# GpSimd makes the low parts of three of the 18 weight units of each expert

## The chip, the cores and the metric

The kernel runs on one core of one Trainium2 chip. The metric is the device time of one execution in microseconds (us), median of several runs. The core has five engines that run side by side and meet through semaphores: TensorE (PE, with its weight loads shown apart as PEld), VectorE (DVE), ScalarE (ACT), GpSimd (POOL) and SyncE (SP, whose queue issues the weight transfers). All arithmetic here is in 32-bit floats.

## The reference

The reference is two transformer blocks over 256 tokens of width 1024. The first block has attention and a dense feed-forward network. The second runs two layers of a hybrid mixer; after the first mixer comes a dense network, after the second a mixture of experts. The change touches that last stage alone:

```python
logits = (x @ router_w).astype(jnp.float32) + router_b.astype(jnp.float32)
top_vals, top_idx = lax.top_k(logits, TOP_K)              # TOP_K = 2 of N_EXPERTS = 8
top_w = jax.nn.softmax(top_vals, axis=-1)
gate = jnp.sum(jax.nn.one_hot(top_idx, N_EXPERTS, dtype=jnp.float32) * top_w[..., None], axis=-2)
out = jnp.zeros_like(x)
for e in range(N_EXPERTS):                                # F_EXPERT = 1408
    out = out + gate[..., e:e + 1] * swiglu(x, w1[e], w3[e], w2[e])
```

where `swiglu(x, w1, w3, w2)` is `(silu(x @ w1) * (x @ w3)) @ w2`.

## The kernel before, in words

**How a product keeps its precision.** Every operand of a matrix product is split into a high part, which TensorE's fast 32-bit format holds exactly, and a low part, the rest. A product is three matmuls: high by high, low by high and high by low (lines 1369 to 1371). ScalarE makes the high part of a weight with a copy (`split_moe` of the scalar engine, line 730), VectorE the low part with a subtraction, raw minus high (`split_moe` of the vector engine, line 1262).

**The units of an expert.** The weights of one expert come in 18 units. Units 0 to 11 are gate and up weights in three chunks of columns, two gate halves and two up halves for each chunk (0 to 3, 4 to 7, 8 to 11). Units 12 to 17 are the down weights, two column halves of three parts. A unit has 2048 columns for each of 128 partitions; units 8 to 11, 14 and 17 have 1536.

**The rings.** Raw weights land in a ring of six places (`RAW_MOE`; three are shown as `raw`, three as `scr`). The high and the low parts have rings of four places each (`W_MOE`; shown as `w_hi` and `w_lo`, and the fourth place as `mt_hi` and `mt_lo`). SP issues the load of unit m, two transfers, once the low part of unit m-6 is made, since then the raw place is free (lines 394 and 395). ScalarE makes the high part of unit m when the load has landed and TensorE has used unit m-4. VectorE makes the low part of m as soon as the high part is there. TensorE waits for the low part of m on the counter `lo_ready` and multiplies (`rows` for units 0 to 11, `down` for 12 to 17).

**The order around the change.** Every engine has the order of its work written out by hand. Within expert e, VectorE does the splits of units 4, 5 and 6, then `gate_up(0)` (line 1280: the activation times the up product), splits 7 and 8, `take_hidden(0)` (line 1292: low part of the turned hidden rows), splits 9 and 10, the next expert's rows (`take_rows`, line 1267), `gate_up(1)`, splits 11 and 12, `take_hidden(1)`, splits 13 and 14, `take_rows`, `gate_up(2)`, splits 15 and 16, `take_hidden(2)`, split 17, `take_y(0)` (line 1305), then splits 0, 1 and 2 of the next expert, `take_y(1)`, and split 3. TensorE multiplies units 0 to 4, turns the hidden rows (`turn_hidden(0)`, line 1834), multiplies 5 and 6, turns half of the next expert's tokens (`turn_gathered`, line 1770), multiplies 7 and 8, `turn_hidden(1)`, 9 and 10, then waits for `take_hidden(1)` and turns the second half of the tokens, then 11, 12, `turn_hidden(2)`, 13, waits for `take_hidden(2)`, and 14 to 17.

**GpSimd before.** In this stage its queue holds the indirect transfer that gathers the tokens of each expert (line 458), and after the last one the load of the gain and bias of the final normalisation (`load_norm(6)`, line 418), which waits until the last expert's tokens are turned. The final normalisation uses them on line 864.

**Sparse and dense.** An expert with at most 128 tokens runs with one tile of gathered tokens, one with more runs over both tiles of all 256 tokens. Each engine reads the count and branches at the start of an expert. In this data seven experts are sparse and expert 6 is dense.

Of the kernel before, what the change touches and what calls it, by code (L numbers as in the profile page):

```python
# [21 lines left out]
F32 = mybir.dt.float32  # L22
F32R = mybir.dt.float32r
U32 = mybir.dt.uint32
ALU = mybir.AluOpType
# [10 lines left out]
EXPERTS = 8  # L36
# [3 lines left out]
RING = 3  # L40
# [13 lines left out]
U_MOE = U_MIX[1] + 27  # L54
# [8 lines left out]
PER_EXPERT = len(EXPERT_UNITS)  # L63
RAW_MOE = 2 * RING
W_MOE = RING + 1
FT = F_EXPERT // P


def unit_width(m):
    kind, c, part = EXPERT_UNITS[m % PER_EXPERT]  # L70
    return DOWN_TILES[part][1] * 512 if kind == "D" else 4 * CHUNKS[c][1]
# [71 lines left out]
def two_blocks(nc, A, const_dram, out):  # L143
    with ExitStack() as ctx:
# [61 lines left out]
        raw_moe = [raw[:, (U_MOE + k) % RING, :] for k in range(RING)] + [area(at, UNIT) for at in (0, 2048, 4096)]  # L206
# [92 lines left out]
        def ev(name):  # L299

            if name not in S:
                S[name] = sem(name)
            return S[name]
# [15 lines left out]
            eng.wait_ge(evacuated[q % 2], q // 2 + 1)  # L319


        def k_major(w):
            return w.rearrange("(k p) n -> p k n", p=P)

        @block.sync
        def _(sp):
            for t in range(TT):
                sp.dma_start(x[:, t, :], A["x"][0, t * P:(t + 1) * P, :]).then_inc(x_landed[t], 16)
            sp.dma_start(ident, const_dram[:, 0:P]).then_inc(ev("ident_landed"), 16)

            def load(u, slot, first, second, width=1024):

                if not (isinstance(u, int) and u < RING):
                    sp.wait_ge(lo_ready, u - RING + 1)
                fill(raw[:, slot, :], raw_landed[slot], first, second, width)

            def fill(place, landed, first, second, width):
                for half, src in ((0, first), (1, second)):
                    dst = place[:, half * width:(half + 1) * width]
                    if len(src.shape) == 3:  # L340
                        dst = dst.rearrange("p (k n) -> p k n", k=src.shape[1])
                    elif len(src.shape) == 4:
                        dst = dst.rearrange("p (e k n) -> p e k n", e=src.shape[1], k=src.shape[2])
                    sp.dma_start(dst, src).then_inc(landed, 16)

            def load_square(u, w, c):
                v = k_major(w)
                load(u, u % RING, v[:, 0:4, c:c + 256], v[:, 4:8, c:c + 256])

            def load_short(u, w, c):  # L350
                v = k_major(w)
                load(u, u % RING, v[:, 0:2, c:c + 512], v[:, 2:4, c:c + 512])

            def load_ffn(u0, wg, wu, wd):
                gv, uv = k_major(wg), k_major(wu)
                with sp.Fori(0, FT_DENSE // 2) as i:
                    for j in range(2):
                        c = bass.ds(i * 256 + j * P, P)
                        load(u0 + j + i * 3, (u0 + j) % RING, gv[:, :, c], uv[:, :, c])
                    load(u0 + 2 + i * 3, (u0 + 2) % RING, wd[bass.ds(i * 256, P), :], wd[bass.ds(i * 256 + P, P), :])  # L360

            for n, (_, c) in enumerate(IN1):
                load_square(U_IN1 + n, A["w_in"][0], c)
            for n in range(4):
                load_square(U_WO + n, A["w_o"][0], n * 256)
            load_ffn(U_FFN1, A["w_gate"][0], A["w_up"][0], A["w_down"][0])
            for l in range(2):
                for n in range(19):
                    load_square(U_MIX[l] + n, A["w_in_2"][l], n * 256)
                for n in range(2):  # L370
                    load_short(U_MIX[l] + 19 + n, A["w_o_attn_2"][l], n * 512)
                for n in range(2):
                    load_short(U_MIX[l] + 21 + n, A["w_o_ret_2"][l], n * 512)
                for n in range(4):
                    load_square(U_MIX[l] + 23 + n, A["w_out_2"][l], n * 256)
                if l == 0:
                    load_ffn(U_FFN2, A["ffn_w1_2"][0], A["ffn_w3_2"][0], A["ffn_w2_2"][0])
            for m in range(PER_EXPERT * EXPERTS):
                e, (kind, c, part) = m // PER_EXPERT, EXPERT_UNITS[m % PER_EXPERT]
                if m < RING:  # L380
                    sp.wait_ge(lo_ready, U_MOE + m - RING + 1)
                elif m == RING:
                    sp.wait_ge(ev("routing"), 1)
                elif m >= RAW_MOE:
                    sp.wait_ge(lo_ready, U_MOE + m - RAW_MOE + 1)
                if kind == "D":
                    at, n = DOWN_TILES[part]
                    v = k_major(A["moe_w2_2"][0, e])[:, at:at + n, c * 512:(c + 1) * 512]
                else:
                    at, n = CHUNKS[c]  # L390
                    v = k_major(A["moe_w1_2" if kind == "G" else "moe_w3_2"][0, e])[:, 4 * part:4 * part + 4, at:at + n]
                rows, width = v.shape[1], v.shape[2]
                dst = raw_moe[m % RAW_MOE][:, 0:rows * width].rearrange("p (k n) -> p k n", n=width)
                sp.dma_start(dst[:, 0:2], v[:, 0:2]).then_inc(raw_moe_landed[m % RAW_MOE], 16)
                sp.dma_start(dst[:, 2:], v[:, 2:]).then_inc(raw_moe_landed[m % RAW_MOE], 16)

            for t in range(TT):
                sp.wait_ge(rows_ready, 2 * 6 + t + 1)
                sp.dma_start(out[0, t * P:(t + 1) * P, :], x[:, t, :]).then_inc(stored, 16)
            sp.wait_ge(stored, 16 * TT)  # L400
# [3 lines left out]
        def _(pool):  # L404
# [46 lines left out]
            for t in range(TT):  # L451
                pool.wait_ge(x_stored[t], 16)
            pool.wait_ge(gb_used, 6)
            for e in range(EXPERTS):
                pool.wait_ge(ev("slots_ready"), 1 if e == 0 else 2)
                if e >= 2:
                    pool.wait_ge(x_turned, 2 * (e - 1))
                pool.indirect_dma_start(x_rows[:, e % 2, :], None, x_dram, bass.IndirectOffsetOnAxis(slot_token[:, e:e + 1], 0)) \
                    .then_inc(rows_gathered[e % 2], 16)
            pool.wait_ge(x_turned, 2 * EXPERTS)  # L460
            load_norm(6)

# [356 lines left out]
        def _(dve):  # L819
# [435 lines left out]
            dve.wait_ge(ev("counts_ready"), 1)  # L1255

            def split_moe(m):
                if m >= PER_EXPERT * EXPERTS:
                    return
                s, width = m % W_MOE, unit_width(m)  # L1260
                dve.wait_ge(hi_ready, U_MOE + m + 1)
                TTo(wl_moe[s][:, 0:width], raw_moe[m % RAW_MOE][:, 0:width], wh_moe[s][:, 0:width].bitcast(F32), ALU.subtract).then_inc(lo_ready, 1)  # L1262
# [102 lines left out]
        def _(pe):  # L1365
# [417 lines left out]
            def expert(e, dense):  # L1783
# [8 lines left out]
                def rows(p):  # L1792

                    kind, c, half = EXPERT_UNITS[p]
                    n, s = CHUNKS[c][1], (e * PER_EXPERT + p) % W_MOE
                    bank = 0 if kind == "G" else (2 if dense else 1)
                    if half == 0 and kind == "G":
                        if c == 0:
                            pe.wait_ge(xg_ready, 2 * e + 2)
                        if e or c:  # L1800
                            pe.wait_ge(silued, 3 * e + c)
                        if e and c == 0 and dense:
                            pe.wait_ge(y_ready, 2 * e)
                    if half == 0 and kind == "U" and (e or c):
                        pe.wait_ge(hid_rows, 3 * e + c)
                        if dense:
                            pe.wait_ge(hid_pair, 3 * e + c)
                        if c == 0:
                            pe.wait_ge(y_ready, 2 * e)
                    pe.wait_ge(lo_ready, u + p + 1)  # L1810
                    for t in range(tiles):
                        tok = slice(t * P, (t + 1) * P)
                        for k in range(4):
                            w = slice(k * n, (k + 1) * n)
                            last = product(ps[:, bank + t, 0:n], xh[4 * half + k][:, tok], xl[4 * half + k][:, tok],
                                           wh_moe[s][:, w], wl_moe[s][:, w], half == 0 and k == 0, half == 1 and k == 3)
                    last.then_inc(unit_used, 1)
# [19 lines left out]
                def down(p):  # L1837
# [1 line left out]
                    _, c, part = EXPERT_UNITS[p]  # L1839
                    s = (e * PER_EXPERT + p) % W_MOE  # L1840
                    first, n = DOWN_TILES[part]
                    pe.wait_ge(lo_ready, u + p + 1)
                    pe.wait_ge(hid_pair, 3 * e + part + 1)
                    if e and not dense and part == 0 and c == 0:
                        pe.wait_ge(y_ready, 2 * e)
# [87 lines left out]
```

## Time and profile before

| what | value |
|---|---|
| median of 3 runs | 1581.41 us (1580.67 to 1583.89) |
| the profiled execution | 1578.89 us |
| its span in the trace | 1577.1 us |
| mean granted TensorE clock | 0.948 of full speed |
| PE busy | 1417.8 us (90% of the span) |
| VectorE busy | 972.1 us (62%) |
| ScalarE busy | 776.3 us (49%) |
| GpSimd busy | 38.1 us (2%) |
| the expert stage | about 1062 to 1562 us of the span |

The span is the time from the first to the last instruction of the trace; the execution's own time is 1.8 us more. Busy time counts computing instructions only, and matmuls overlap, so that a busy TensorE isn't one at its peak. A row of a timeline gives start, duration, engine, line, output and inputs; in square brackets stands the idle time of that engine just before it and what ended it.

### The profile page before, as it was taken

The numbers are of one execution on the slowest core, as the hardware profiler recorded it, in microseconds if no ns is written. First come the engines' busy times: TensorE is split into PE (matmuls) and PEld (weight loads), VectorE is DVE, ScalarE is ACT, GpSimd is POOL, SyncE is SP. The second block draws the span as 40 slices with busy tenths as digits, with TensorE's granted clock in tenths as the row PEclk, the third lists the DMA queues.
The fourth block names the chain that finished last, engine by engine and source line by source line (L and its number), as shares of the span: only waits on it lengthen the run. The fifth ranks groups of instructions, "written<-read, shape, count | busy, mean of one in ns | idle before, by whom it ended". The sixth has DMA issues, their size and how long they took to land.

```text
span 1577.1 us, 21924 instructions
## 1 busy us (share of the span) xinstructions
PE 1417.8 (90%) x8969; PEld 1282.8 (81%) x8969; DVE 972.1 (62%) x953; ACT 776.3 (49%) x784; POOL 38.1 (2%) x59
## 2 busy tenths in 40 slices
PE   4996899997999988999979999869999999889975
PEld 4985899996999977999969998757777777778864
DVE  5585654556446775455564467658688888664556
ACT  3663345443554433445436454317566666544353
POOL 1000000001000000000000000010000000000000
PEclk9997999998999998999979999969899999999998
DMA  8432466665445345656644443368899999775761
GB/s 255 160 108 54 134 186 187 185 186 140 137 155 153 112 138 148 193 170 183 198 129 140 149 151 96 121 226 288 273 359 318 321 328 346 256 259 172 235 192 63
DMA packets 249343, 299.84 MB, mean 190 GB/s; under 512 B 10016, under 2 KB 180128, under 8 KB 249120
## 3 DMA queue, kind: packets, MB, share of 16 engines
q1 hardware_dynamic: 244688, 283.22, 55.5%
q0 software_dynamic: 4560, 15.27, 3.5%
q8 instruction: 70, 1.15, 0.3%
q14 instruction: 25, 0.20, 0.0%
HBM read 296.35 MB, written 2.10 MB: 189 GB/s over the span
## 4 chain that ended last, share of the span: by engine, by line
PE 79%; DVE 14%; ACT 4%; issue 2%; DMA 1%; SPq 0%; ACTq 0%; DVEq 0%
PE ps L1369 21%; PE ps L1370 20%; PE ps L1371 20%; DVE w_lo L1262 3%; PE ps L1564 3%; PE ps L1565 3%; PE ps L1566 3%; ACT w_hi L730 2%; DVE w_lo L826 1%; DMA raw<-in_w_in_dram 1%; PE ps L1653 1%; PE ps L1634 1%; DVE x L864 1%; DVE x L865 1%; DVE small L839 1%
## 5 line engine op out<-in xcount | busy, mean ns | idle before, releaser
L826 DVE TENSOR_TENSOR w_lo<-raw,w_hi 128x2048 fp32r<-128x2048 f32 x139 | 317.9, 2291 | 232.7 <-ACT w_hi L474 232.7
L474 ACT ACTIVATE w_hi<-raw 128x2048 fp32r<-128x2048 f32 x139 | 264.9, 1907 | 192.8 <-PE ps L1371 119.0
L1369 PE MATMUL ps<-xt_hi,w_hi 128*128 128x256 f32 x912 | 263.2, 289 | 15.8 <-DVE xt_lo L875 15.8
L1370 PE MATMUL ps<-xt_lo,w_hi 128*128 128x256 f32 x912 | 262.0, 287 | 0.0
L1371 PE MATMUL ps<-xt_hi,w_lo 128*128 128x256 f32 x912 | 261.6, 287 | 0.0
L1369 PE MATMUL ps<-w_hi,xt_hi 128*128 128x256 f32 (+3 forms) x808 | 240.8, 298 | 5.8 <-DVE xt_lo L835 3.1
L1370 PE MATMUL ps<-w_lo,xt_hi 128*128 128x256 f32 (+3 forms) x808 | 237.7, 294 | 0.0
L1371 PE MATMUL ps<-w_hi,xt_lo 128*128 128x256 f32 (+3 forms) x808 | 237.7, 294 | 0.0
L1369 PEld LDWEIGHTS ps<-xt_hi,w_hi 128*128 128x128 f32 x912 | 179.2, 197 | 19.7 <-issue 18.8
L1370 PEld LDWEIGHTS ps<-xt_lo,w_hi 128*128 128x128 f32 x912 | 179.3, 197 | 0.8
L1371 PEld LDWEIGHTS ps<-xt_hi,w_lo 128*128 128x128 f32 x912 | 179.1, 196 | 0.0
L1369 PEld LDWEIGHTS ps<-w_hi,xt_hi 128*128 128x128 f32 x808 | 157.6, 195 | 12.0 <-issue 6.3
L1370 PEld LDWEIGHTS ps<-w_lo,xt_hi 128*128 128x128 f32 x808 | 157.7, 195 | 2.0
L1371 PEld LDWEIGHTS ps<-w_hi,xt_lo 128*128 128x128 f32 x808 | 157.6, 195 | 2.1
L1262 DVE TENSOR_TENSOR w_lo<-raw,w_hi 128x2048 fp32r<-128x2048 f32 (+1 forms) x57 | 121.8, 2141 | 39.1 <-ACT w_hi L730 38.7
L1262 DVE TENSOR_TENSOR w_lo<-scr,w_hi 128x2048 fp32r<-128x2048 f32 (+1 forms) x48 | 99.3, 2069 | 72.2 <-ACT w_hi L730 72.2
L730 ACT ACTIVATE w_hi<-raw 128x2048 fp32r<-128x2048 f32 (+1 forms) x57 | 102.0, 1794 | 44.7 <-PE ps L1371 44.7
L730 ACT ACTIVATE w_hi<-scr 128x2048 fp32r<-128x2048 f32 (+1 forms) x48 | 83.3, 1736 | 74.3 <-PE ps L1371 74.3
L1369 PE MATMUL ps<-w_hi,xg_hi 128*128 128x512 f32 (+1 forms) x252 | 98.6, 391 | 20.5 <-issue 18.7
L1370 PE MATMUL ps<-w_lo,xg_hi 128*128 128x512 f32 (+1 forms) x252 | 96.8, 384 | 0.0
L1371 PE MATMUL ps<-w_hi,xg_lo 128*128 128x512 f32 (+1 forms) x252 | 96.5, 383 | 0.0
L592 ACT ACTIVATE scr<-ps 128x256 f32<-128x256 f32 x44 | 16.9, 384 | 121.5 <-PE ps L1371 121.5
(350 smaller groups left out, 2453.5 us busy)
## 6 DMA issues: line engine op xcount, KB each, us to landing
raw<-in_moe_w_dram SPq DMA_DIRECT2D x120, 512.0 KB, 5.2
raw<-in_w_in_dram SPq DMA_DIRECT2D x100, 512.0 KB, 4.7
scr<-in_moe_w_dram SPq DMA_DIRECT2D x88, 512.0 KB, 6.6
raw<-in_ffn_w_dram SPq DMA_DIRECT2D x66, 512.0 KB, 4.3
scr<-in_moe_w_dram SPq DMA_DIRECT2D x48, 384.0 KB, 3.9
raw<-in_w_gate_dram SPq DMA_DIRECT2D x22, 512.0 KB, 4.0
raw<-in_w_up_dram SPq DMA_DIRECT2D x22, 512.0 KB, 5.2
raw<-in_w_down_dram SPq DMA_DIRECT2D x22, 512.0 KB, 4.2
```

The costliest lines, as they stand in the source:

```text
L474: A_(w_hi[:, slot, :], raw[:, slot, :], ACT.Copy).then_inc(hi_ready, 1)
L592: A_(silu_t[:, j, :], ps[:, (s0[1] + j) % 2, 0:T], ACT.Silu).then_inc(silu_ready, 1)
L730: A_(wh_moe[s][:, 0:width], raw_moe[k][:, 0:width], ACT.Copy).then_inc(hi_ready, 1)
L826: TTo(w_lo[:, slot, :], raw[:, slot, :], w_hi[:, slot, :].bitcast(F32), ALU.subtract).then_inc(lo_ready, 1)
L839: return nc.vector.bn_stats(stats[:, t, c, :], x[:, t, c * 512:(c + 1) * 512])
L1262: TTo(wl_moe[s][:, 0:width], raw_moe[m % RAW_MOE][:, 0:width], wh_moe[s][:, 0:width].bitcast(F32), ALU.subtract).then_inc(lo_ready, 1)
L1369: MM(dst, a_hi, b_hi, start=start, stop=False)
L1370: MM(dst, a_hi, b_lo, start=False, stop=False)
L1371: return MM(dst, a_lo, b_hi, start=False, stop=stop)
L1564: MM(dst, h_hi_t[:, j, tok], w_hi[:, s, w], start=False, stop=False)
L1565: MM(dst, h_hi_t[:, j, tok], w_lo[:, s, w], start=False, stop=False)
L1566: last = MM(dst, h_lo_t[:, j, tok], w_hi[:, s, w], start=False, stop=False)
```

## The change

VectorE no longer makes the low parts of units 5, 11 and 17 of each expert; GpSimd makes them, with the same subtraction. They count on a semaphore of their own (`pool_low`), and SP and TensorE wait for the one or the other by a new helper. On GpSimd's queue the gather of the tokens of expert e+1 now stands in front of the three subtractions of expert e, and so behind those of expert e-1; before it only waited for tokens to be turned. Reads and writes are the same data in the same places.

```diff
+POOL_LOW = (5, 11, 17)
+
+def by_pool(m):
+    return RING < m < PER_EXPERT * EXPERTS and m % PER_EXPERT in POOL_LOW
+
+def low_count(m):
+
+    return sum(by_pool(i) == by_pool(m) for i in range(m + 1))
...
+        def wait_low(eng, m):
+
+            if by_pool(m):
+                eng.wait_ge(ev("pool_low"), low_count(m))
+            else:
+                eng.wait_ge(lo_ready, U_MOE + low_count(m))
...
                 elif m >= RAW_MOE:
-                    sp.wait_ge(lo_ready, U_MOE + m - RAW_MOE + 1)
+                    wait_low(sp, m - RAW_MOE)
...
-            for e in range(EXPERTS):
+            def fetch_rows(e):
                 pool.wait_ge(ev("slots_ready"), 1 if e == 0 else 2)
                 if e >= 2:
                     pool.wait_ge(x_turned, 2 * (e - 1))
                 pool.indirect_dma_start(x_rows[:, e % 2, :], None, x_dram, bass.IndirectOffsetOnAxis(slot_token[:, e:e + 1], 0)) \
                     .then_inc(rows_gathered[e % 2], 16)
+
+            def split_low(m):
+                s, width = m % W_MOE, unit_width(m)
+                pool.wait_ge(hi_ready, U_MOE + m + 1)
+                nc.gpsimd.tensor_tensor(wl_moe[s][:, 0:width], raw_moe[m % RAW_MOE][:, 0:width],
+                                        wh_moe[s][:, 0:width].bitcast(F32), ALU.subtract).then_inc(ev("pool_low"), 1)
+
+            fetch_rows(0)
+            for e in range(EXPERTS):
+                if e + 1 < EXPERTS:
+                    fetch_rows(e + 1)
+                for k in POOL_LOW:
+                    split_low(e * PER_EXPERT + k)
             pool.wait_ge(x_turned, 2 * EXPERTS)
             load_norm(6)
...
             def split_moe(m):
-                if m >= PER_EXPERT * EXPERTS:
+                if m >= PER_EXPERT * EXPERTS or by_pool(m):
                     return
...
-                    pe.wait_ge(lo_ready, u + p + 1)
+                    wait_low(pe, e * PER_EXPERT + p)
```

The last pair of lines stands twice, in `rows` and in `down`.

## Rows read from the trace of the kernel before

**Rows 1.** The page: busy time of each engine, and the chain by engine.
```profile
PE 1417.8 (90%) x8969; PEld 1282.8 (81%) x8969; DVE 972.1 (62%) x953; ACT 776.3 (49%) x784; POOL 38.1 (2%) x59
PE 79%; DVE 14%; ACT 4%; issue 2%; DMA 1%; SPq 0%; ACTq 0%; DVEq 0%
```

**Rows 2.** Waits of TensorE, 1062 to 1562 us: total, times, longest.
```profile
PE ps L1369 <- issue: 19.5, 9, 8.3
PE ps L1369 <- DVE h_lo_m L1292: 12.6, 7, 1.8
```

**Rows 3.** Chain that ended last, 1200 to 1218 us: start, duration, what.
```profile
1202.14 1.93 ACT w_hi L730
...
1204.09 2.29 DVE w_lo L1262
1206.39 0.61 DVE h_lo_m L1292
...
1207.04 0.66 PE ps L1770 x4
```

**Rows 4.** Timeline of expert 2 around its unit 11: ScalarE, then VectorE.
```profile
1200.05 1.49 ACT L730 ACTIVATE mt_hi<-scr 128x1536 fp32r<-128x1536 f32 x1 [1.27 <-PE ps L1371]
1201.58 1.76 DVE L1262 TENSOR_TENSOR mt_lo<-scr,mt_hi 128x1536 fp32r<-128x1536 f32 x1 [0.23 <-ACT mt_hi L730]
```

**Rows 5.** Timeline of expert 2: high part of unit 5, low part of 6, then.
```profile
1181.90 1.91 ACT L730 ACTIVATE w_hi<-scr 128x2048 fp32r<-128x2048 f32 x1
1187.14 2.29 DVE L1262 TENSOR_TENSOR w_lo<-raw,w_hi 128x2048 fp32r<-128x2048 f32 x1 [1.00 <-ACT w_hi L730]
1189.35 0.74 DVE L1280 SCALAR_TENSOR_TENSOR const<-ps,small,scr 128x512 f32<-128x512 f32 x1
1190.53 0.60 PE L1834 MATMUL ps<-const 128*128 128x128 f32 x4
```

**Rows 6.** The queue of GpSimd: timeline.
```profile
1.94 0.56 POOL L421 MEMSET zeros<- 128x512 f32 x1
1057.67 2.78 POOL L458 DMA_INDIRECT gb<-x_dram,slot_token  x1 [4.75 <-DVE slot_token L1254]
1061.10 0.94 POOL L458 DMA_INDIRECT gb<-x_dram,slot_token  x1 [0.65 <-issue]
1154.64 1.59 POOL L458 DMA_INDIRECT gb<-x_dram,slot_token  x1 [58.91 <-PE ps L1770]
```

**Rows 7.** VectorE beside two of those transfers: timeline.
```profile
1057.30 2.29 DVE L1262 TENSOR_TENSOR mt_lo<-scr,mt_hi 128x2048 fp32r<-128x2048 f32 x1
1153.13 2.29 DVE L1262 TENSOR_TENSOR mt_lo<-raw,mt_hi 128x2048 fp32r<-128x2048 f32 x1
```

**Rows 8.** Expert 0 around its unit 5: ScalarE, VectorE, TensorE.
```profile
1068.96 1.91 ACT L730 ACTIVATE w_hi<-scr 128x2048 fp32r<-128x2048 f32 x1
1073.11 2.29 DVE L1262 TENSOR_TENSOR w_lo<-raw,w_hi 128x2048 fp32r<-128x2048 f32 x1
L1834 PE MATMUL ps<-const x4: 272/272/273, 1076.2 to 1076.5; 128*128 128x128 f32 x4
```

**Rows 9.** Dense expert 6: VectorE's low parts of its units 6 and 12.
```profile
1421.94 2.29 DVE L1262 TENSOR_TENSOR w_lo<-raw,w_hi 128x2048 fp32r<-128x2048 f32 x1 [3.27 <-ACT w_hi L730]
1454.23 2.29 DVE L1262 TENSOR_TENSOR w_lo<-raw,w_hi 128x2048 fp32r<-128x2048 f32 x1 [2.85 <-ACT w_hi L730]
```

**Rows 10.** Expert 2: high part of unit 17, VectorE's first split behind it.
```profile
1215.81 1.48 ACT L730 ACTIVATE w_hi<-scr 128x1536 fp32r<-128x1536 f32 x1 [0.84 <-PE ps L1371]
1222.34 2.29 DVE L1262 TENSOR_TENSOR w_lo<-raw,w_hi 128x2048 fp32r<-128x2048 f32 x1 [1.11 <-ACT w_hi L730]
```

**Rows 11.** Chain that ended last, 1530 to 1577 us: start, duration, what.
```profile
1544.06 4.44 DVE w_lo L1262 x2
...
1568.70 1.30 DVE x L864
```

**Rows 12.** Transfers of 1175 to 1229 us: count, KB each, us to landing.
```profile
scr<-in_moe_w_dram SPq DMA_DIRECT2D x11, 512.0 KB, 6.9
```

More of the change, by code:

```diff
@@ L1841, in down @@
                     first, n = DOWN_TILES[part]
-                    pe.wait_ge(lo_ready, u + p + 1)
+                    wait_low(pe, e * PER_EXPERT + p)
                     pe.wait_ge(hid_pair, 3 * e + part + 1)
```

## The prediction

> **What bounds the kernel now.** I read the page first: TensorE is busy 90% of the span, VectorE 62%, GpSimd 2%, and 79% of the chain that ended last is TensorE [rows 1]. A lighter VectorE is worth something only where TensorE waits for it. The waits of TensorE in the expert stage show where: each of the seven sparse experts has one wait of up to 1.8 us for line 1292, the low part of the turned hidden rows; the rest is mostly "issue", at the starts of experts [rows 2]. The chain inside one expert then shows what stands ahead of such a wait: high part of unit 12, 1202.14 to 1204.07, its low part from 1204.09 to 1206.38, line 1292, and TensorE again at 1207.04 [rows 3]. The reader is to see that the low part of unit 12 starts 0.02 us after its high part has ended: VectorE was waiting for ScalarE, and ScalarE for TensorE to free a place of the ring. The last step was to look at what VectorE does just before it: the low part of unit 11 (one of the three that move) ends at 1203.34, and VectorE is then idle for 0.75 us [rows 4]. It is the same for unit 5: the low part of unit 6 has 1.00 us of idle time before it, ended by ScalarE [rows 5]. And VectorE's first split behind unit 17 is preceded by 1.11 us of idle time [rows 10].
>
> So what is taken off VectorE was followed by a pause each time, and no row has TensorE waiting because of it. The removal itself is worth nothing.
>
> **The change part by part.** *Removed:* 24 subtractions on VectorE, three per expert: one of 2048 columns (2.29 us) and two of 1536 (1.76 us), 5.81 us per expert, 46 us in all. On the path: 0, by the above.
>
> *Added: the price of one split on GpSimd.* The trace shows no two-input operation there. Below, it can't be expected to beat VectorE's own 2.29 us by a row. The nearest GpSimd row is the clearing of 128x512 in 0.56 us [rows 6], 1.09 ns per column for one stream. Three streams, one after another (two read, one written), would be 2048 x 3 x 1.09 ns = 6.69 us; two, if the write goes along with the reads, 4.46 us. I take 4.46 us, that row's rate once for each of the two inputs; it also lies in the middle of 2.29 and 6.69. For 1536 columns three quarters: 3.34 us, bounds 1.76 and 5.02.
>
> *Is such a split late by itself?* Unit 11: its high part ends at 1201.54, GpSimd would end at 1204.9; TensorE can't use it before the turning at 1207.04 is over [rows 3, 4]. With 5.02 us it would be 1206.6, still in time. Unit 5: high part done at 1183.81, GpSimd ends at 1188.3, at worst at 1190.5; TensorE comes to it after the turning that starts at 1190.53 [rows 5]. Unit 17: high part done at 1217.29, GpSimd done at 1220.6 [rows 10], while four units of down weights stand between it and its use. None is late.
>
> *Does it hold up VectorE?* This is the term that decides. When the kernel before asks GpSimd for an indirect transfer, which reads its list of rows from the on-chip memory, its duration depends on VectorE. With no split running it is 0.94 us (1061.10). Issued at 1057.67, while VectorE subtracts from 1057.30 to 1059.59, it takes 2.78 us and ends at 1060.45, which is 0.86 us behind the end of that subtraction. Issued at 1154.64, during the one from 1153.13 to 1155.42, it takes 1.59 us and ends 0.81 us behind [rows 6, 7]. Six such issues stand beside a split and all end 0.8 to 0.9 us after it. GpSimd's read waits, then, until the whole two-input subtraction is over. I take it that the wait works the other way round too: a subtraction of VectorE that comes while GpSimd subtracts starts when GpSimd has finished. VectorE's other work here (lines 1280, 1292, 1267, 1305) has one input in the accumulators and I count it as free.
>
> The Trainium skill, "SBUF — State Buffer", section "SBUF: two separate sides", says it outright: VectorE and GpSimd share a pair of ports under an exclusive lock, the first holds it for its whole instruction, and a VectorE operation with two inputs in that memory needs it against a GpSimd operation that reads. The rows show one direction of this; no row shows VectorE as the one that waits. The "GPSIMD Engine Reference", section "Elementwise — side-by-side cycle accounting", states 4497 ns for a two-input operation of 2048 columns; by that the sum below would be 13.5 instead of 13.0 us.
>
> *Unit 11.* GpSimd starts at 1201.58 and ends at 1204.92. The low part of unit 12 would start at 1204.09, so it is held for 0.83 us, and it is on the chain: line 1292 and TensorE's turning move by 0.83 us. Expert 7 turns no further tokens, but there the chain runs through VectorE's queue behind the same split, down to the splits that end at 1548.50 [rows 11], so it pays the same. Seven sparse experts: 7 x 0.83 = 5.8 us.
>
> *Unit 5.* GpSimd works from 1183.85 to 1188.31; the low part of unit 6 is due at 1187.14 and held for 1.17 us. Queued behind it on VectorE is line 1280, now 1189.35 to 1190.09, then 1190.52 to 1191.26. TensorE's turning waits for that: with some 0.1 us of handing over it starts at 1191.36 instead of 1190.53 [rows 5], 0.83 us late. Six experts: 5.0 us. In expert 0 the high part of unit 5 comes late, at 1070.87, so GpSimd holds until 1075.36 and the low part of unit 6 is late by 2.25 us; the turning follows its line 1280 with 0.1 us of room [rows 8]: 2.2 us.
>
> *Unit 17.* GpSimd is done at 1220.6, and the next split of VectorE is due at 1222.34 [rows 10]: 0.
>
> *Dense expert 6.* TensorE takes twice as long per unit, and the low parts of units 6 and 12 stand behind 3.27 and 2.85 us of idle time [rows 9], that is 5.56 and 4.61 us behind the starts of 5 and 11, more than 4.46 and 3.34: 0.
>
> *Moved.* SP's loads wait for the low parts. The load of unit 11 goes out 2.2 us later (4.46 against 2.29). Before, it was issued when unit 5 was done, at about 1186.1, lands in 6.9 us [rows 12] and is wanted at 1200.05 [rows 4]: 7 us of room. The two narrow ones move by 1.6 us. Behind it in SP's queue stand the loads of the following units with the same room. The gathers of tokens come up to an expert later, behind unit 17 of the expert before; each moves 128 rows of 4 KB, 512 KB, as much as one transfer that lands in 6.9 us [rows 12], and the rows are turned from the seventh unit of the next expert on, some 20 us later. The final gain and bias now wait for unit 17 of expert 7. VectorE's splits of 15 and 16 end at 1548.50 there, unit 17 follows on GpSimd from about 1549.0 to 1552.4, and with 1.2 us of issue and 7 us of landing the rows are there at 1560.6, wanted at 1568.70 [rows 11]. All 0, with 8 us of room in the last; that room is gone only if GpSimd takes three times what I think.
>
> *Sum.* 5.8 + 5.0 + 2.2 = 13.0 us slower. On the profiled execution (span 1577.1, own time 1578.89) that is 1591.9; the median of the runs is 2.5 us above it, 1581.41, and 1594.4 is what I forecast.
>
> **The rivals.** *A, no blocking:* GpSimd's subtraction doesn't hold up VectorE's. For it: the rows show only GpSimd waiting, never VectorE. Against it: the wait in the one direction is for a whole instruction, which looks like a lock. Then every term above is 0 and the time is 1581.4. This is the case on the other side (not slower); it decides at the first split of unit 12. *B, blocking, and GpSimd takes 6.69 and 5.02 us:* unit 11 holds unit 12 until 1206.60, 2.51 us, seven times, 17.6; unit 5 holds unit 6 for 3.40, of which 0.34 is hidden, 3.06 six times, 18.4; expert 0 pays 4.4. Together 40.4, 1621.8. *C, the two share:* VectorE's split is only slowed while both run, say by half of what I price: 6.5 us, 1587.9. *D, faster:* TensorE's waits at expert starts are uneven, up to 8.3 us and 19.5 us in nine of them [rows 2]; if the later gathers leave these starts quieter, a few us come back, 5 perhaps, which only shows as faster if nothing blocks: 1576.4.
>
> **How the numbers follow.** The forecast has 0.62, A 0.17, C 0.08, B 0.06, D 0.07. What a measurement of this kernel can tell is about 0.2%, 3.2 us. My own forecast reaches from 1589 to 1603: a price of 4.0 to 5.0 us, a tenth of a us of handing over at each of 14 stalls, and stretches at TensorE's lower clock, whose granted mean is 0.948 and which longer pauses could make more frequent. A lies inside the range and B mostly outside: 1580.5 to 1604. Slower by over 0.2%: the forecast, B and C, less what of C and the forecast falls short, 0.73. Within 0.2%: A and that remainder, 0.19. Faster: D and a bit of A, 0.08.
>
> **What would show it.** In the profile after: 24 rows of GpSimd of about 4.5 and 3.3 us; in the sparse experts the low part of unit 12 starts not 0.02 but about 0.85 us after its high part, right at the end of GpSimd's split; the wait for line 1292 before the turning of tokens grows by 0.8 us; TensorE waits for line 1280 before the first turning of hidden rows. The forecast is wrong if VectorE's splits overlap GpSimd's with their usual 2.29 us (A), or if one of GpSimd's is the last thing that TensorE waits for (B).

## The result, and the profile after

The changed kernel takes 1598.62 us (median of 7 runs, 1591.84 to 1602.39), the kernel before in the same sittings 1581.41 (7 runs, 1571.87 to 1590.22). The ratio is 1.0102, with a 95% interval from 1.0066 to 1.0138: slower by 16 us, give or take 6. The profiled execution has a span of 1597.8 us, 20.7 more than before.

The page after: busy times and the chain by engine, beside [rows 1]. VectorE lost 30 us of busy time where 46 were taken off it; the other 16 are waits that count as busy, as the timeline below shows. GpSimd went from 38 to 128.5 us, and the chain has less TensorE and more VectorE.

```profile
PE 1424.2 (89%) x8969; PEld 1286.6 (81%) x8969; DVE 941.9 (59%) x929; ACT 777.3 (49%) x784; POOL 128.5 (8%) x83
PE 75%; DVE 15%; ACT 5%; issue 4%; DMA 1%; SPq 0%; ACTq 0%; DVEq 0%
```

GpSimd's new work, two of its four groups by shape and place: count, total us, mean ns. A whole unit takes 4.65 us, a narrow one 3.51.

```profile
L484 POOL TENSOR_TENSOR w_lo<-scr,w_hi 128x1536 fp32r<-128x1536 f32 x8 | 28.1, 3511 | 122.7 <-ACT w_hi L763 122.7
L484 POOL TENSOR_TENSOR mt_lo<-scr,mt_hi 128x2048 fp32r<-128x2048 f32 x4 | 18.6, 4650 | 96.6 <-ACT mt_hi L763 96.6
```

Timeline of expert 2 of the changed kernel, first around unit 5, then around unit 11; it answers to [rows 4, 5].

```profile
1188.41 4.66 POOL L484 TENSOR_TENSOR w_lo<-scr,w_hi 128x2048 fp32r<-128x2048 f32 x1 [16.98 <-ACT w_hi L763]
1191.67 3.55 DVE L1295 TENSOR_TENSOR w_lo<-raw,w_hi 128x2048 fp32r<-128x2048 f32 x1 [4.24 <-ACT w_hi L763]
1195.14 0.74 DVE L1313 SCALAR_TENSOR_TENSOR const<-ps,small,scr 128x512 f32<-128x512 f32 x1
1195.94 0.66 PE L1867 MATMUL ps<-const 128*128 128x128 f32 x4 [0.71 <-DVE const L1313]
...
1207.09 3.53 POOL L484 TENSOR_TENSOR mt_lo<-scr,mt_hi 128x1536 fp32r<-128x1536 f32 x1 [14.02 <-ACT mt_hi L763]
1209.57 3.21 DVE L1295 TENSOR_TENSOR w_lo<-raw,w_hi 128x2048 fp32r<-128x2048 f32 x1 [2.75 <-ACT w_hi L763]
...
1213.43 0.66 PE L1803 MATMUL ps<-const,gb 128*128 128x128 f32 x4 [1.29 <-DVE h_lo_m L1325]
```

The hold is there, but it looks otherwise than I had said. VectorE's split doesn't start late, it starts when it is due (0.03 us behind the high part) and lasts longer: the instruction is recorded while it waits. The sum gives it away. GpSimd ends at 1193.07 and VectorE at 1195.22, 2.15 us later; GpSimd ends at 1210.62 and VectorE at 1212.78, 2.16 us later. In both cases all but 0.14 us of the 2.29 us that this split takes with nothing beside it [rows 3] comes after GpSimd has finished.

TensorE's waits of the changed kernel in the expert stage: total, times, longest. They answer to [rows 2].

```profile
PE ps L1402 <- issue: 20.1, 7, 8.4
PE ps L1402 <- DVE h_lo_m L1325: 12.6, 7, 1.8
PE ps L1803 <- DVE h_lo_m L1325: 7.7, 6, 1.3
PE ps L1867 <- DVE const L1313: 7.2, 8, 2.1
...
PE ps L1402 <- DVE w_lo L1295: 2.1, 1, 2.1
```

The kernel before has one more row that is needed beside [rows 2], for the turning of tokens:

```profile
PE ps L1770 <- DVE h_lo_m L1292: 2.3, 6, 0.4
```

The seven waits of 1.8 us stand as they were. New are 0.9 us more in each of six waits before the turning of tokens (behind unit 12; 0.38 us each before), and eight before the turning of hidden rows: six of 0.7, one of 2.1 in expert 0, and one of 0.8 in expert 7, which comes down VectorE's queue from unit 12. The last row is a pause at the start of an expert like those marked "issue": it is put down to the split that came last, though the one that TensorE needed there had ended over 2 us before. Pauses at starts are counted with both rows from here on: 19.5 us before, 22.2 after.

### The profile page after: what moved, and what is told of

Same layout as the page of the kernel before. It is cut to its first block, busy times and chain, and to the rows that moved or that the text cites. A ratio compares the mean times of both kernels' runs of the same rounds, so it can differ in the third digit from the quotient of the medians.

```text
span 1597.8 us, 21926 instructions
## 1 busy us (share of the span) xinstructions
PE 1424.2 (89%) x8969; PEld 1286.6 (81%) x8969; DVE 941.9 (59%) x929; ACT 777.3 (49%) x784; POOL 128.5 (8%) x83
## 4 chain that ended last, share of the span: by engine, by line
PE 75%; DVE 15%; ACT 5%; issue 4%; DMA 1%; SPq 0%; ACTq 0%; DVEq 0%
PE ps L1402 20%; PE ps L1403 19%; PE ps L1404 19%; DVE w_lo L1295 3%; ACT w_hi L763 3%; PE ps L1597 3%; PE ps L1598 3%; PE ps L1599 2%; DVE w_lo L859 2%; DMA raw<-in_w_in_dram 1%; PE ps L1686 1%; PE ps L1667 1%; DVE x L897 1%; DVE x L898 1%; DVE small L872 1%
## 5 line engine op out<-in xcount | busy, mean ns | idle before, releaser
L1295 DVE TENSOR_TENSOR w_lo<-raw,w_hi 128x2048 fp32r<-128x2048 f32 (+1 forms) x57 | 137.8, 2428 | 85.7 <-ACT w_hi L763 85.6
L1295 DVE TENSOR_TENSOR w_lo<-scr,w_hi 128x2048 fp32r<-128x2048 f32 (+1 forms) x36 | 76.0, 2112 | 66.1 <-ACT w_hi L763 66.1
L1402 PEld LDWEIGHTS ps<-w_hi,xg_hi 128*128 128x128 f32 x252 | 49.0, 194 | 34.4 <-issue 24.5
```

The source lines that it names most:

```text
L1402: MM(dst, a_hi, b_hi, start=start, stop=False)
```

## The experiments

Each is compared with the kernel before, run beside it on the same chip.

**Nothing left but the move.** One line of the changed kernel:

```diff
-                s, width = m % W_MOE, unit_width(m)
+                s, width = m % W_MOE, 8
```

> The changed kernel, but GpSimd's three subtractions per expert cover 8 columns instead of the whole unit, so most of the low parts of units 5, 11 and 17 are missing. Everything else of the change stays: the lighter VectorE, the second semaphore, the gathers behind the subtractions. Theory H (VectorE's next split is held while GpSimd subtracts, and that is the whole loss): no hold is left, 1581 us, and the low part of unit 12 takes 2.29 us again. Rival M (a good part of the loss comes from what was moved, the gathers and loads): stays slower, 1586 to 1598. Rival R (the removal itself is worth something that the hold hides): faster than before by more than 3 us.

Measured 1579.03 us beside 1578.75: ratio 1.0000 (0.9976 to 1.0024). TensorE's waits by VectorE are those of before, and the split of 2048 columns takes 2.29 us on average (3 per expert are missing on VectorE). So neither the removal nor the moved gathers and the second semaphore are worth anything that shows, to within 4 us either way; that one hides the other can't be excluded by the time alone, but no wait of TensorE speaks for it. Rival M falls. Rival R, faster by more than 3 us, keeps only the edge of the interval.

**One unit at a time.** The changed kernel with one line changed, `POOL_LOW = (11,)`, `(5,)` and `(17,)`.

> Only unit 11 of each expert goes to GpSimd. Theory H: the low part of unit 12 shows some 3.2 us instead of 2.29 in the seven sparse experts, 7 x 0.92 = 6.4 us, 1588; unit 6 untouched, 2.29. Rival M: the time hardly depends on which unit moved. Rival L (GpSimd's own low part comes late for TensorE): TensorE waits for GpSimd's line.

> Only unit 5 of each expert goes to GpSimd. Theory H: the low part of unit 6 shows 3.55 us, TensorE waits about 0.75 us for the activation product before it turns hidden rows in six experts and about 2 us in expert 0: 6 to 7 us, 1588. Rival M: as for unit 11.

> Only unit 17 of each expert goes to GpSimd. VectorE's next split starts after GpSimd has finished, so theory H: nothing is held, 1581 us, though a third of the work was moved and the gathers and the last norm's loads stand behind it as in the change. Rival M: slower by 3 us or more, since all that was moved is here too.

Unit 11: ratio 1.0069 (1.0045 to 1.0093), 11 us. Unit 5: 1.0055 (1.0035 to 1.0075), 9 us. Unit 17: 1.0018 (0.9997 to 1.0039), not told from no change. In the trace each has exactly its own waits: with unit 11 alone 7.7 us before the turning of tokens and 0.8 in expert 7; with unit 5 alone 6.3 us before the turning of hidden rows; with unit 17 neither. Unit 11 and unit 5 cost more than their waits, 5.4 + 0.8 and 6.3 us, by 2 to 5 us; for unit 11 that is just outside the interval. Added up the three make 22 us, where the whole change has 16 (10 to 22): no more can be read from the sum.

**The unit that is on the chain.** `POOL_LOW = (16,)`.

> Only unit 16 of each expert goes to GpSimd, the one whose low part stands between TensorE's unit 12 and the low part of the turned hidden rows, for which TensorE waits 1.8 us in each sparse expert. Theory H with the reading that a move pays only where VectorE is on the chain: line 1325 no longer queues behind that split, the seven waits of 1.8 us go, VectorE's split of unit 17 is held for about 2 us but has room: 12.6 us faster than before, 1566. Rival G (any subtraction on GpSimd costs here, by power, clock or loads): slower than before, 1583 or more. Rival N (unit 16 now late for TensorE): the wait moves to GpSimd's line, 1575 to 1581.

Ratio 1.0021 (0.9997 to 1.0045): no gain. The waits for line 1325 before unit 14 are gone, all seven. Timeline of expert 2 in this kernel, GpSimd and VectorE:

```profile
1216.28 4.63 POOL L484 TENSOR_TENSOR w_lo<-scr,w_hi 128x2048 fp32r<-128x2048 f32 x1 [48.60 <-ACT w_hi L763]
1216.60 0.56 DVE L1325 TENSOR_TENSOR h_lo_m<-ps,h_hi_m 128x384 fp32r<-128x384 f32 x1 [0.79 <-ACT h_hi_m L792]
1218.93 3.60 DVE L1295 TENSOR_TENSOR w_lo<-scr,w_hi 128x1536 fp32r<-128x1536 f32 x1 [1.77 <-ACT w_hi L763]
```

Two things can be read here. Line 1325, with one input in the accumulators (`ps`), ran in its usual 0.55 us in the middle of GpSimd's subtraction, here and in the other six sparse experts: it isn't held. The split of 1536 columns behind it was held to 1220.91 and took 1.62 us more, again 0.14 less than its usual 1.76. And the time? The pauses at the starts of experts grew from 19.5 us [rows 2] to this:

```profile
PE ps L1402 <- issue: 28.3, 9, 7.6
```

That is 8.8 of the 12.6 us. My theory's 1566 is wrong. The time, 1580.37 us, lies in rival N's range, but not for its reason: no wait for GpSimd's line appears. The wait went away where I said, and came back in a place that neither theory had. Rival G, 1583 or more, lies at the edge of the interval; what speaks against it is that GpSimd's subtractions of unit 17, alone, cost nothing that shows either.

**The same wait removed without GpSimd.** On ScalarE and VectorE of the kernel before:

```diff
-                split_moe(m + 16)
                 take_hidden(2)
+                split_moe(m + 16)
```

> The kernel before, and nothing on GpSimd; on ScalarE and VectorE alike the hidden rows' third part (take_hidden(2)) now stands in front of the split of unit 16 instead of behind it. If the chain of the profile is right, the seven waits of 1.8 us go and nothing takes their place: 12.6 us faster, 1566. Rival: the split of unit 16 becomes late by what it was moved, 0.5 us, and TensorE waits for it instead: at least half of the gain is lost, 1573 or more.

1571.79 us, ratio 0.9965 (0.9947 to 0.9983): 5.5 us faster and not 12.6. Again the seven waits are gone, and the pauses at starts are 25.6 us (23.7 as "issue", 1.9 as line 1262), 6.1 more. The rival was right that over half of the gain is lost, but not in the reason: TensorE never waits for the split of unit 16. This is the fastest kernel here that keeps the branches, and it beats both kernels of this case. In the changed kernel the same exchange:

> The changed kernel with the same exchange of take_hidden(2) and split 16. Theory H: the holds of units 6 and 12 lie elsewhere and stay, so the exchange brings the same 12 us as in the kernel before: 1598 - 12.6 = 1586 beside 1594 to 1598 for the changed kernel. Rival: the holds were partly hidden in that wait, and without it they cost more, so less than 8 us come back.

Ratio 1.0003 (0.9982 to 1.0025), where the changed kernel has 1.0102: it brings some 16 us, give or take 7, so the 12.6 us of waits that it removes lie within. The holds stay (7.8 and 7.2 us of waits), so the rival falls, and the pauses at starts are 22.0 us, as in the changed kernel. In the two profiles the difference is 20.3 us; 12.6 are waits, and the granted clock from 1080 to 1500 us is 0.99 here and 0.96 in the changed kernel. Set beside the exchange in the kernel before, which ran next to it, the change costs some 6 us here (1577.70 against 1571.79) and not 16, although it adds the same waits, 5.5 and 7.2 us: the pauses at starts are 3.6 us shorter, and the granted clock is 0.99 against 0.97.

**Writing without reading.** GpSimd clears the place instead of subtracting:

```diff
...
-                nc.gpsimd.tensor_tensor(wl_moe[s][:, 0:width], raw_moe[m % RAW_MOE][:, 0:width],
-                                        wh_moe[s][:, 0:width].bitcast(F32), ALU.subtract).then_inc(ev("pool_low"), 1)
+                low = wl_moe[s][:, 0:width].bitcast(F32)
+                for i in range(2):
+                    done[0] += 1
+                    nc.gpsimd.memset(low, 0.0).then_inc(pool_step, 1)
+                    pool.wait_ge(pool_step, done[0])
+                nc.gpsimd.memset(low[:, 0:8], 0.0).then_inc(ev("pool_low"), 1)
```

> The changed kernel, but on GpSimd each subtraction is replaced by two clearings of the same place one after the other and one of 8 columns: it writes about as long (3.5 to 4.5 us for 2048 columns, by 0.56 us for 512) but reads nothing; the low parts of units 5, 11 and 17 are zero. If what holds VectorE is GpSimd's reading: no split of VectorE is longer than 2.29 us, 1579 to 1581. If any GpSimd work holds it: the low part of unit 6 and of unit 12 show 2.5 to 3.3 us and the time is 1585 to 1595.

Ratio 1.0005 (0.9982 to 1.0029). The clearings were faster than I had worked out, so in most experts they reach only 0.3 to 0.4 us into VectorE's split. In expert 0, where the high part of unit 5 comes late, they reach further. Expert 0 around unit 5, then expert 2 around unit 11:

```profile
1068.88 3.68 POOL L489 MEMSET w_lo<- 128x2048 f32 x2 [10.23 <-ACT w_hi L769]
1070.75 2.29 DVE L1301 TENSOR_TENSOR w_lo<-raw,w_hi 128x2048 fp32r<-128x2048 f32 x1 [3.31 <-ACT w_hi L769]
...
1200.46 2.83 POOL L489 MEMSET mt_lo<- 128x1536 f32 x2 [13.92 <-ACT mt_hi L769]
1202.96 2.29 DVE L1301 TENSOR_TENSOR w_lo<-raw,w_hi 128x2048 fp32r<-128x2048 f32 x1 [2.75 <-ACT w_hi L769]
```

They overlap by 1.81 and 0.33 us, and the split takes 2.29 both times. GpSimd at work, and writing to the same place as before, doesn't hold VectorE; what the subtraction has beyond that is the reading. One long overlap and thirteen short ones show it, and that it is the reading and not another trait of that instruction is an inference.

**Without the branches.** To see what the pauses at the starts are, TensorE, ScalarE and VectorE lose the read of the count and the jump (TensorE's lines; the other two have the same):

```diff
-                n = pe.value_load(counts8[0:1, e:e + 1], min_val=0, max_val=T)
-                with pe.If(n > SLOTS):
-                    expert(e, True)
-                with pe.Else():
-                    expert(e, False)
+                expert(e, e == 6)
```

> The kernel before without its branches: TensorE, ScalarE and VectorE don't read the token counts, expert 6 is written as the dense one and the others as sparse, so the code of an expert follows that of the last one without a jump. It fits only this routing and serves to take the jumps away. Theory J (the waits marked issue at the starts of experts come from the jump and the code behind it): the five of 0.8 to 3.8 us and the one of 8.3 us go, 18 us, 1561. Rival W (they come from the weights being late): they stay, 1576 or more.

> The kernel before with take_hidden(2) in front of split 16 (run e6_swap_before) and without the branches. With the branches the exchange removed seven waits of 1.8 us and brought 5.5 us, while the waits at the starts of experts grew. Theory J: without jumps the whole 12 us show, 1549 beside 1561 for the straight kernel before. Rival W: again only about half, 1555.

> The changed kernel without the branches. Theory H: the holds stand inside the experts, so they cost what their waits add up to in the trace, 13 to 14 us more than the straight kernel before: 1574.5. Rival: part of the 16 us came by way of longer pauses at the starts or of a lower clock, and the difference is under 10 or over 17 us.

| kernel | median us | ratio to before |
|---|---|---|
| straight, before | 1554.74 | 0.9853 (0.9828 to 0.9879) |
| straight, exchange | 1534.50 | 0.9718 (0.9694 to 0.9743) |
| straight, changed | 1562.60 | 0.9889 (0.9864 to 0.9915) |

The waits of the straight kernel before, beside [rows 2]:

```profile
PE ps L1361 <- DVE h_lo_m L1288: 12.6, 7, 1.8
PE ps L1762 <- DVE h_lo_m L1288: 2.3, 6, 0.4
PE ps L1361 <- DVE y_lo L1301: 2.3, 1, 2.3
PE ps L1361 <- issue: 2.0, 2, 1.5
```

"issue" fell from 19.5 to 2.0 us: the pauses came from the branch, that is the read of the count, the jump and the code behind it, which no run here takes apart. Theory J's cause holds, its numbers don't: all three kernels came out 6 to 15 us below what was expected. The kernel before gained 24 us, more than the pauses were. Some 4 us of the rest are clock: by the clock rows of the traces TensorE works 25 us of the expert stage at 1.2 GHz in the kernel before, 17.5 in the straight one. Without jumps the exchange brings about 20 us instead of 5.5, and the change costs 6 to 8 us instead of 16, under 10 as the rival of the third run has it. Both differ from the 12.6 us of waits that the exchange removes and the change adds, one up, one down, and the granted clock of TensorE accounts for most of that. One row of the stretch from 1080 to 1500 us for each of the three (busy us of each engine, then the granted clock, the share of the transfers and GB/s), in the order of the table:

```profile
1080.00:1500.00 420.00, 404.03 (x1872) 337.05 (x1871) 309.97 (x206) 256.44 (x195) 8.77 (x7) 0.98 0.87 297
```

```profile
1080.00:1500.00 420.00, 415.07 (x1960) 349.41 (x1958) 323.71 (x216) 269.35 (x205) 8.77 (x7) 1.00 0.89 309
```

```profile
1080.00:1500.00 420.00, 394.68 (x1853) 328.73 (x1854) 278.91 (x184) 252.78 (x193) 84.07 (x27) 1.00 0.85 294
```

The straight kernel before had 0.98 of full speed there, the other two 1.00 (with the exchange one stretch of 3.4 us at the lower clock is left, at 1366.9). Its timeline shows where it was lost. TensorE in expert 1, behind one of the waits of 1.8 us:

```profile
1157.19 0.48 PE L1361 MATMUL ps<-w_hi,h_hi_m 128*128 128x512 f32 x1 [1.82 <-DVE h_lo_m L1288]
...
1158.69 0.63 PE L1362 MATMUL ps<-w_lo,h_hi_m 128*128 128x512 f32 x1
1159.12 0.63 PE L1363 MATMUL ps<-w_hi,h_lo_m 128*128 128x512 f32 x1
...
1162.09 0.40 PE L1363 MATMUL ps<-w_hi,h_lo_m 128*128 128x512 f32 x1
1162.32 0.40 PE L1361 MATMUL ps<-w_hi,h_hi_m 128*128 128x512 f32 x1
```

Matmuls start 0.43 us apart, and 0.23 apart from 1161 on: 1.2 GHz for some 3.4 us, then 2.4 again, 1.7 us lost. The same happens in the next three experts, each time right behind that wait. The exchange removes the wait and with it this stretch: 12.6 us and about 7 make the 20. The straight changed kernel has the same waits and more, and yet not one such stretch between 1080 and 1500 us; it pays 12.6 us in waits and saves some 7 here and 2 more at the start of the stage; 2 to 4 of the 6 to 8 us measured stay open. It isn't a matter of one execution: all six runs of the straight kernel before have a mean clock between 0.945 and 0.949, all six of the straight changed kernel one between 0.953 and 0.956. Why the kernel with more pauses kept the higher clock, no run here explains.

**Taking the held split off the chain.** In the changed kernel, on ScalarE and VectorE:

```diff
-                split_moe(m + 12)
                 take_hidden(1)
+                split_moe(m + 12)
```

> The changed kernel with take_hidden(1) in front of the split of unit 12 on ScalarE and VectorE (behind it before). The hold of unit 12 stays as long as it is, 0.9 us, but line 1325 and TensorE's turning no longer queue behind it. Theory H: the six waits of 1.3 us before the turning go, 7.7 us, and the low part of unit 12 is still in time for TensorE; about 1590 where the changed kernel has 1597, or a little less of it if the starts of experts take some back. Rival: what is held is late for TensorE anyway, and the wait moves to the low part of unit 12: no gain.

1592.23 us, ratio 1.0084 (1.0058 to 1.0111) against 1.0102 for the changed kernel: its own interval doesn't tell the two apart. In the trace the six waits of 1.3 us are gone and nothing of VectorE's took their place (2.4 us of "issue" before a turning did), so the split of unit 12 was in time. But the hold didn't stay, as theory H had it. Expert 2, GpSimd's unit 11 and VectorE's unit 12:

```profile
1205.95 3.53 POOL L484 TENSOR_TENSOR mt_lo<-scr,mt_hi 128x1536 fp32r<-128x1536 f32 x1 [14.04 <-ACT mt_hi L763]
1209.29 2.35 DVE L1295 TENSOR_TENSOR w_lo<-raw,w_hi 128x2048 fp32r<-128x2048 f32 x1 [1.11 <-ACT w_hi L763]
```

ScalarE now makes the high part of unit 12 later, so the split starts only 0.19 us before GpSimd ends and is held for 0.06 us instead of 0.92. The exchange did two things at once, and what it would bring with the hold still there isn't shown. The pauses at starts are 24.1 us, 1.9 more. The direction is theory H's, the size isn't shown.

## Why the prediction was right

*The removal is worth 0.* Right, measured with GpSimd's work cut to 8 columns: 1.0000, to within 0.0024.

*GpSimd's price.* 4.46 and 3.34 us were predicted, 4.65 and 3.51 measured. The lower bound of 2.29 and rival B's 6.69 were both far off. The rate of the clearing as I used it was high for large tiles (2048 columns are cleared in 1.81 us, 0.88 ns per column, not 1.09), so that two streams at the true rate would have given 3.6; the number came out well partly by luck.

*None of GpSimd's parts is late.* Right: TensorE never waited for line 484.

*VectorE is held in its turn.* Right. It was the one step taken over from the other direction, and it is now shown by the durations: 3.55 us for unit 6, 3.21 for unit 12. The Trainium skill, "SBUF — State Buffer", section "SBUF: two separate sides", had it so, the lock for the whole instruction included; by that the trace agrees, with VectorE's end 2.15 us behind GpSimd's. The traces add a measure. Where GpSimd starts first, whether the two overlap by 0.19, 0.68, 1.05, 1.40, 1.98 or 2.81 us, VectorE's split is longer by the overlap less 0.14 us. That rules out A, in which nothing is held, and C, in which the two share. B falls by the durations of 4.65 and 3.51 us and because TensorE never waited for GpSimd.

*Where the chain was read.* The wait at 1207.04 [rows 3], before the turning of tokens, isn't one of the waits of 1.8 us, as the prediction has it. It is one of six of 0.38 us; those of 1.8 us stand behind the split of unit 16, as the runs on that unit show. For the sum it made no difference: TensorE was already waiting at 1207.04, so what unit 12 was held came through whole.

*Unit 11, 5.8 us.* Measured in waits: 5.4 us in six experts and 0.8 in expert 7, 6.2. *Unit 5, 7.2 us.* Measured 6.4: the hold is 1.26 us and not 1.17, but the room before the turning was larger than I had taken, so 0.7 and not 0.83 us come through in each; expert 0 paid 2.1 of 2.2. *Unit 17, dense expert, moved loads and gathers:* 0, right. In expert 6 the splits of units 6 and 12 take 2.29 us. The last gain and bias are issued at 1573.3 and wanted at 1589.4. The sum in waits is 12.6 us where I had 13.0.

*The time.* 1594.4 us was forecast, 1598.6 measured; 16 us (10 to 22) slower and not 13. The rest of the profiled difference, 20.7 less 12.6, lies in the two items that I had put into the range and not into the sum: the pauses at the starts of experts, 2.7 us longer, and what is then left, 5 us, stretches at the lower clock (the mean is 0.939 after and 0.948 before; by the clock rows TensorE works 25 us of the stage at 1.2 GHz before and 36 us after, at half speed 5 us lost). That they are no fixed part of the change is what the other forms of the kernel show, where the same waits cost 6 to 8 us. So the mechanism and the 12.6 us of waits are what the prediction got right; that the whole time lay so near is in part luck. Rival D had the pauses shrink; they moved in both directions from kernel to kernel.

*What I said it would look like.* The start of the low part of unit 12 stayed 0.03 us behind its high part and the wait went into its duration. A reader who had looked for my sign alone, the late start, would have called the hold absent.

## What to carry to other kernels

Work taken off an engine pays only where that engine is what the path waits for at that point: look at whether an idle time stands between the moved instruction and the next one. Before giving GpSimd a subtraction that reads two tensors from the on-chip memory, look at when VectorE's next instruction with both inputs in that memory is due (with one in the accumulators it wasn't held here); if that is sooner than GpSimd's duration, VectorE waits for the rest, and the wait is found in the duration of its instruction, not before it. A wait that is removed may come back elsewhere: here a reordering of two lines was worth 5.5 us with branches and 20 without, and a change that adds 12.6 us of waits cost 16, 6 or 8 us, depending on what stood around it.

## What was not expected of the hardware

The pauses of TensorE at the starts of experts depend on what goes before. In the kernel before those of experts 1 to 5 are 3.34, 0.84, 0.92, 1.17 and 0.31 us, and a second one of 3.82 us stands within the first unit of expert 5; with the exchange of line 1292 and split 16, where TensorE reaches the end of each expert about 1.8 us sooner, they are 2.79, 2.76, 1.94, 2.96 and 2.78, and the second one of expert 5 is 3.53. Without the branch they are absent. That the branch makes them is shown; what sets their length wasn't tried.

GpSimd's indirect transfers, 0.94 us alone and 1.2 to 2.8 beside a split of VectorE [rows 6, 7], are all 0.95 us in the changed kernel where they follow GpSimd's own subtraction of unit 17, a moment at which no split of VectorE runs:

```profile
1170.47 0.95 POOL L478 DMA_INDIRECT gb<-x_dram,slot_token  x1
1227.41 0.95 POOL L478 DMA_INDIRECT gb<-x_dram,slot_token  x1 [0.15 <-issue]
```
